# Other order, other PSUM banks and other group sizes in the seven-product up blocks of a hybrid decoder step

## What is computed

```python
def _swiglu(h, w_in, w_out):
    a, b = jnp.split(h @ w_in, 2, axis=-1)
    return (jax.nn.silu(a) * b) @ w_out
...
for i in range(DEPTH):
    x = x + 0.5 * _swiglu(_rmsnorm(x, ln_ffn1[i]), ffn1_w_in[i], ffn1_w_out[i])
    x = x + mixer_i(_rmsnorm(x, ln_mix[i]))
    x = x + 0.5 * _swiglu(_rmsnorm(x, ln_ffn2[i]), ffn2_w_in[i], ffn2_w_out[i])
return _rmsnorm(x, ln_final)
```

## Time and profile before

| | |
|---|---|
| runs (3) | 2259.43, 2260.98, 2261.5 us; median 2260.98 |
| profiled execution | 2256.29 us, span 2254.6 us |
| mean granted TensorE clock | 0.991 |
| busy of the span | PE 97%, VectorE 66%, ScalarE 37% |
| first fast up and down blocks | about 841 to 1243 us of the span |
| second fast up and down blocks | about 1839 to 2240 us |

### The profile page before, as it was taken

How to read it: one execution, slowest core, us unless ns; L and a number is a source line. 1 busy time by engine, 2 the same in 40 slices (tenths; PEclk the granted TensorE clock), 3 DMA queues, 4 the chain that set the end, 5 groups by cost and what they waited for, 6 DMA issues and landing times. The chain is left out here.

```text
span 2254.6 us, 43269 instructions
## 1 busy us (share of the span) xinstructions
PE 2187.2 (97%) x17624; PEld 2148.8 (95%) x17624; DVE 1481.9 (66%) x2218; ACT 828.9 (37%) x1134; POOL 2.2 (0%) x15
## 2 busy tenths in 40 slices
PE   9999999999999789999999999999989999999998
PEld 9999999999999788999999999999988989999998
DVE  5767775467877679758577675234358569668485
ACT  4222232334454445425244322122243345335153
POOL 0000000000000000000000000000000000000000
PEclk9999999999999999999999999999999999999999
DMA  4324543332323225535232322332274424324132
GB/s 137 93 81 121 146 124 96 95 95 72 102 63 91 64 65 142 146 86 143 80 108 61 94 76 78 89 94 76 87 198 159 118 71 132 107 84 141 54 95 81
DMA packets 426648, 227.91 MB, mean 101 GB/s; under 512 B 33473, under 2 KB 419730, under 8 KB 426514
## 3 DMA queue, kind: packets, MB, share of 16 engines
q1 hardware_dynamic: 413986, 212.98, 33.9%
q10 hardware_dynamic: 12528, 13.08, 1.7%
HBM read 206.91 MB, written 23.30 MB: 102 GB/s over the span
## 5 line engine op out<-in xcount | busy, mean ns | idle before, releaser
L2460 PE MATMUL ps<-h_hi,w_hi 128*128 128x288 f32 x1920 | 418.9, 300 | 3.7 <-DVE w_lo L1454 1.9
L2460 PE MATMUL ps<-h_hi,w_lo 128*128 128x288 f32 x1920 | 410.9, 296 | 0.0
L2460 PE MATMUL ps<-h_lo,w_hi 128*128 128x288 f32 x1920 | 410.7, 295 | 0.0
L2592 PE MATMUL ps<-hf_hi,s_hi 128*128 128x288 f32 x1232 | 366.7, 298 | 20.1 <-issue 9.1
L2592 PE MATMUL ps<-hf_lo,s_hi 128*128 128x288 f32 x1232 | 363.0, 295 | 0.0
L2592 PE MATMUL ps<-hf_hi,s_lo 128*128 128x288 f32 x1232 | 362.7, 294 | 0.0
L2460 PEld LDWEIGHTS ps<-h_hi,w_hi 128*128 128x128 f32 x1920 | 308.1, 189 | 13.7 <-issue 5.9
L1454 DVE TENSOR_TENSOR w_lo<-w_raw,w_hi 128x2048 fp32r<-128x2048 f32 (+4 forms) x155 | 267.8, 1731 | 77.4 <-ACT w_hi L911 75.7
L911 ACT ACTIVATE w_hi<-w_raw 128x2048 fp32r<-128x2048 f32 (+4 forms) x155 | 225.9, 1462 | 233.7 <-PE ps L2460 222.5
L2460 PEld LDWEIGHTS ps<-h_lo,w_hi 128*128 128x128 f32 x1920 | 309.2, 189 | 0.0
L2460 PEld LDWEIGHTS ps<-h_hi,w_lo 128*128 128x128 f32 x1920 | 309.1, 189 | 0.0
(11 more groups left out here) (413 smaller groups left out, 3116.4 us busy)
## 6 DMA issues: line engine op xcount, KB each, us to landing
s_raw<-in_ffn_w_in_dram SPq DMA_DIRECT2D x220, 256.0 KB, 3.3
w_raw<-in_ffn_w_in_dram SPq DMA_DIRECT2D x88, 512.0 KB, 5.0
w_raw<-in_hgrn_w_in_dram SPq DMA_DIRECT2D x32, 512.0 KB, 5.4
w_raw<-in_ffn_w_out_dram SPq DMA_DIRECT2D x64, 256.0 KB, 3.1
w_raw<-in_ffn_w_out_dram SPq DMA_DIRECT2D x32, 384.0 KB, 3.9
w_raw<-in_ffn_w_out_dram SPq DMA_DIRECT2D x32, 320.0 KB, 3.6
w_raw<-in_s_w_glu_dram SPq DMA_DIRECT2D x16, 512.0 KB, 5.2
w_raw<-in_ffn_w_out_dram SPq DMA_DIRECT2D x32, 192.0 KB, 2.7
```

The lines of the kernel that those rows point to most:

```text
L2460: ins = M.matmul(ps[:, 2 * b + h, 0:HALF], w[j][:, at:at + P], v[:, k, h * HALF:(h + 1) * HALF], start=k == 0 and n == 0, stop=k == ph.kt ...
L2592: ins = M.matmul(out, w, h, start=f in (0, 1, 3) and k == 0 and n == 0, stop=f in (3, 5, 6) and k == KP - 1 and n == 2, skip_group_check=True)
```

## The change

- Groups of 6, 8, 8 units in place of 8, 8, 6.
- Even units use banks 0, 6, 7, odd ones 3, 1, 2. The second product of a group's first units waits for no down tile any more; the first product of a fast down block now also waits for the last unit's `upper_sum`, which reads banks 1 and 2.
- Last unit of a group: `lower_sum` goes ahead of the split of the down weights, which is parted: buffer 0 behind `lower_sum`, buffer 1 behind `gate_rest`.
- First unit: root and reciprocal go behind `upper_sum`, the token sums behind product 4, ScalarE makes all high parts of the next unit ahead of the Silu.
- Units 0, 1 and 22: sums and rests are moved to earlier tiles of the block before (unit 0: tiles 2 to 6 of `hgrn_out`; its rests of groups 2, 3 and those of unit 22 no longer stand in `form_tile`).
- Fast down blocks have functions of their own, unrolled: the scaling is done in place in PSUM, then the addition frees the banks, and the weights of tile m+2 are split behind the addition of tile m.
- The spreading of taps (`spread_taps`, 8 DMAs each) is shared out 4 and 4 over the first two groups, in place of 6 and 2.

```diff
@@ -42,7 +42,7 @@
 F_GROUPS = (12, 10)
-FAST_GROUPS = (8, 8, 6)
+FAST_GROUPS = (6, 8, 8)
...
@@ -533,7 +533,7 @@
         N_FORM = 2 * KP + 1
-        BANKS = ((0, 1, 2), (3, 6, 7))
+        BANKS = ((0, 6, 7), (3, 1, 2))
...
@@ -554,7 +554,7 @@
         def upper_sums(v):
-            return ps[:, 1:3, 0:HALF] if v % 2 == 0 else ps[:, 6:8, 0:HALF]
+            return ps[:, 6:8, 0:HALF] if v % 2 == 0 else ps[:, 1:3, 0:HALF]
...
@@ -816,9 +816,9 @@
                         load_unit(v)
-                        if v - 2 < 6:
+                        if v < 6:
                             spread_taps(v - 2)
-                        elif 10 <= v < 12:
+                        elif 8 <= v < 12:
...
@@ -1014,13 +1014,14 @@
                         gate_high(vl - 1)
-                    if nxt is not None:
+                    if nxt is not None and v % UNITS:
...
                     if v % UNITS == 0:
+                        unit_high(nxt, 0)
...
@@ -1029,12 +1030,14 @@
                         unit_high(nxt, 2)
+                        if v % UNITS == 0:
+                            unit_high(nxt, 3)
...
                         gate_high(vl)
-                    if nxt is not None:
+                    if nxt is not None and v % UNITS:
...
@@ -1185,13 +1188,12 @@
                     taken = (free[j], i + (ph.tile0 + 1))
-                    if ph.fast:
-                        taken = (x_added, i * 2 + (x_at[ph.name] + j + 1))
                     if r in FORMED:
-                        if (i, j) == (ph.pairs - 1, 1):
-                            for g in range(4):
-                                unit_high(FORMED.index(r) * UNITS, g)
-                        form_tile(r, i * 2 + j, taken)
+                        m = i * 2 + j
+                        if m in (3, 5):
+                            unit_high(0, m - 3)
+                            unit_high(0, m - 2)
+                        form_tile(r, m, taken)
...
@@ -1213,6 +1215,17 @@
+            def fast_down(n, ph):
+                r = MAKES.get((ph.kind, ph.name))
+                for m in range(NK):
+                    i, j = divmod(m, 2)
+                    if m + 2 < NK:
+                        split(ph, j, i + 1, ph, i)
+                    elif m + 2 == NK and n + 1 < len(PH) and not into_sup(n):
+                        split(PH[n + 1], 0, 0, ph, None)
+                    if r is not None:
+                        norm_tile(r, m, (free[j], i + (ph.tile0 + 1)))
...
@@ -1401,13 +1414,12 @@
                         unit_high(UNITS, 0)
-                        unit_high(UNITS, 1)
...
                     if last and j == 1:
-                        unit_high(UNITS, 2)
-                        unit_high(UNITS, 3)
+                        for g in range(1, 4):
+                            unit_high(UNITS, g)
...
@@ -1566,44 +1572,71 @@
+                def normalised(v):
                     dve.wait_ge(post_done, 3 * v + 2)
                     V.tensor_tensor(fca[:], fca[:], rstd[:], ALU.mult).then_inc(post_done, 1)
...
+                def first_unit(v):
+                    if v:
+                        sum_three(v + 1)
+                    unit_rest(v + 1, 0)
+                    if v:
+                        sum_fourth(v + 1)
+                    lower_sum(v)
+                    unit_rest(v + 1, 1)
+                    upper_sum(v)
+                    reciprocal(FORMED[v // UNITS])
+                    normalised(v)
+                    unit_rest(v + 1, 2)
+                    unit_rest(v + 1, 3)
...
                     if v % UNITS == 0:
-                        sum_second(nxt)
-                        reciprocal(FORMED[v // UNITS])
-                        lower_sum(v)
-                        unit_rest(nxt, 0)
-                        sum_fourth(nxt)
-                        upper_sum(v)
-                        unit_rest(nxt, 1)
-                        unit_rest(nxt, 2)
-                        unit_rest(nxt, 3)
+                        first_unit(v)
...
                     if nxt is not None:
-                        sum_second(nxt)
+                        sum_three(nxt)
...
                         unit_rest(nxt, 1)
+                    lower_sum(v)
...
                         rest(down_ph, 0, 0)
-                        rest(down_ph, 1, 0)
-                    lower_sum(v)
                     upper_sum(v)
+                    normalised(v)
...
                         gate_rest(vl)
+                        rest(down_ph, 1, 0)
...
+            def fast_down(n, ph):
+                r = MAKES.get((ph.kind, ph.name))
+                if r is not None:
+                    clear_ssq(r)
+                for m in range(NK):
+                    i, j = divmod(m, 2)
+                    dve.wait_ge(full[j], i + (ph.tile0 + 1))
+                    V.tensor_tensor(pair(j), pair(j), halves(rstd[:]), ALU.mult).then_inc(down_scaled, 1)
+                    dve.wait_ge(down_scaled, x_at[ph.name] + m + 1)
+                    V.scalar_tensor_tensor(out=halves(cols(x, m)), in0=pair(j), scalar=-0.5, in1=halves(cols(x, m)),
+                                           op0=ALU.mult, op1=ALU.add).then_inc(free[j], 1)
+                    if m + 2 < NK:
+                        rest(ph, j, i + 1)
+                    elif m + 2 == NK and n + 1 < len(PH) and not into_sup(n):
+                        rest(PH[n + 1], 0, 0)
+                    if r is not None:
+                        norm_tile(r, m)
...
@@ -2035,19 +2068,19 @@
                     m = i * 2 + j
-                    if r in FORMED and m == NK - 1:
-                        unit_ahead(FORMED.index(r) * UNITS)
+                    if r in FORMED:
+                        if m == 2:
+                            sum_three(0)
+                            sum_fourth(0)
+                        elif m in (4, 6):
+                            unit_rest(0, m - 4)
+                            unit_rest(0, m - 3)
+                        elif m == NK - 1:
+                            sum_three(1)
+                            sum_fourth(1)
                     dve.wait_ge(full[j], i + (ph.tile0 + 1))
-                    if ph.fast:
-                        if j or not isinstance(i, int) or i or x_at[ph.name]:
-                            dve.wait_ge(x_added, i * 2 + (x_at[ph.name] + j))
-                        V.tensor_tensor(halves(ft_s[:]), pair(j), halves(rstd[:]), ALU.mult).then_inc(free[j], 1)
-                        dve.wait_ge(free[j], i + (ph.tile0 + 1))
-                        V.scalar_tensor_tensor(out=cols(x, m), in0=ft_s[:], scalar=-scale, in1=cols(x, m),
-                                               op0=ALU.mult, op1=ALU.add).then_inc(x_added, 1)
-                    else:
-                        V.scalar_tensor_tensor(out=halves(cols(x, m)), in0=pair(j), scalar=scale,
-                                               in1=halves(cols(x, m)), op0=ALU.mult, op1=ALU.add).then_inc(free[j], 1)
+                    V.scalar_tensor_tensor(out=halves(cols(x, m)), in0=pair(j), scalar=scale,
+                                           in1=halves(cols(x, m)), op0=ALU.mult, op1=ALU.add).then_inc(free[j], 1)
...
@@ -2388,7 +2421,11 @@
                     if m == NK - 1:
-                        unit_ahead(UNITS)
+                        sum_three(UNITS)
+                        unit_rest(UNITS, 0)
+                        sum_fourth(UNITS)
+                        for g in range(1, 4):
+                            unit_rest(UNITS, g)
...
@@ -2563,7 +2603,7 @@
                         if f in (0, 2, 4, 6):
-                            pe.wait_ge(s_lo_done, 4 * v + (f // 2 + 1 if formed else (1, 2, 4, 4)[f // 2]))
+                            pe.wait_ge(s_lo_done, 4 * v + f // 2 + 1)
...
@@ -2572,8 +2612,6 @@
                                 pe.wait_ge(post_done, 3 * (v - 2) + 2)
-                            else:
-                                pe.wait_ge(free[1], ph.tile0)
...
@@ -2593,7 +2631,7 @@
                         ins.then_inc(prod_done, 1)
-                        if f == 2 and not formed:
+                        if f == 3 and not formed:
...
@@ -2664,6 +2702,8 @@
                     pe.wait_ge(sd_done, 1)
+                if ph.fast:
+                    pe.wait_ge(post_done, 3 * (FAST.index(ph.name[0]) * UNITS + ph.f0 + ph.kt - 1) + 2)
```

23 lines of the change are left out of this document (11 added, 12 removed).

## The result

The changed kernel takes 2234.03 us (median of 4 runs, 2233.6 to 2239.3) beside 2260.20 us (4 runs) of the kernel before in the same measurement: ratio 0.9889, 95% interval 0.9872 to 0.9906. The forecast was 2237 us, its range 2230 to 2247.

A forecast was written before the change was run, and what follows sets the result against it. TensorE, busy for 97% of the span, was taken as the bound, so only its waits and lost clock could be won. 8.3 + 5.1 + 5.9 + 4.6 = 23.9 us off 2261.0 gave 2237 us, range 2230 to 2247.

The forecast's parts named there:

- What bounds it: Whole kernel: TensorE is busy for 97% of the span, so only its waits or lost clock can be won back.
- Ends of groups, 8.3: Four group ends: product 7 no longer waits for `fc`, 8.9 us, less 0.6 charged for the first down product.
- The rival of 2249: Group ends: the wait only moves to the first down product and its second weights; 2249 us, chance 0.10.
- The clock, 5.1: Three low-clock stretches, two behind group-end waits, one behind the `w_lo` wait at 1245.97, go with those waits: 5.1 us gained.
- The rival that it isn't repeated: Whole kernel: the clock gain is not repeated, as the gate falls at other waits; 2242 us, chance 0.14.
- Down blocks and entry, 5.9: Last down blocks and entry of the next up block: `w_lo` waits and slower starts behind them go, 4.5 and 1.4 us.
- its wide bounds: Fast down tiles: in-place scaling in PSUM taken as 0.76 us from the nearest row, with an upper end of 3.76.
- First units, 4.6: First units: product 3 to product 3 falls to 14.1 us from 17.1 and 15.7, gaining 3.0 and 1.6.
- Now, with F the start of product 3: First units: new chain from product 3 through sums, reciprocal, multiplication, Silu and snapshot to the next product 3, 14.1 us.
- F unchanged, with waits of 1.0 and 0.7: `hgrn_out`: new waits at tiles 4 and 6, yet unit 0's product 3 starts as before, within up to 2 us.
- the 844: End of `hgrn_out`: last addition forecast at 843.3; later than about 844 would show the prediction wrong.
- Against the median: Whole kernel: gain taken from the three-run median, 2261.0 us, 4.7 above the profiled execution's 2256.3.

The follow-up runs named there:

- x2_down: Kernel before with only the new fast down blocks (in-place scaling, weight rest behind the addition), groups still 8, 8, 6: 2254.59 us, ratio 0.9981.
- x3_first: Kernel before with only the new order of the first units (reciprocal behind both sums, token sums behind product 4): 2258.64 us, ratio 0.9997.
- y4_ends: Changed kernel with the order at group ends undone, both rests of the down weights ahead of `lower_sum`: 2245.01 us, ratio 0.9938.
- x1_ends: Kernel before with only `lower_sum` put ahead of the split of the down weights, which is parted, at group ends: 2247.85 us, ratio 0.9959.
- y1_sizes: Changed kernel with groups of 8, 8, 6 again and the taps spread as before: 2234.41 us, ratio 0.9893.
- u2_down: Changed kernel with the old fast down blocks (scaled copy in a buffer, weight rest last), groups still 6, 8, 8: 2236.27 us, ratio 0.9887.
- z2_snap: Changed kernel with the next unit's first snapshot ahead of the Silu and `lower_sum` ahead of a rest, in first units: 2234.79 us, ratio 0.9889.
- y2_banks: Changed kernel with the old PSUM banks and the old waits for them: 2235.57 us, ratio 0.9893.

## Why the prediction was right

**What bounds it:** right. Only TensorE's waits and clock moved. Its busy time fell by 4.7 us of the 22.4. The stretches at the lower clock add up to 38.9 us in the trace of before and 32.9 in that of after, so the clock's loss fell from 19.5 to 16.5, 3.0 us.

**Ends of groups, 8.3, and 3.4 of clock behind two of them:** right in place, size and sum (11.7 forecast; 9.3 to 11.7 alone, 11.0 undone, 12.0 in the traces). The order on DVE came out as drawn, and the wait did not move to the first down product. The rival of 2249 falls. The 0.15 charged at each end for the banks is below what can be measured.

**The clock, 5.1:** the three stretches named did go, with some luck; one of 1.7 came in `hgrn_out`, which the text did not foresee. The rival that it isn't repeated asked how often a wait of 2.1 us at a group's end is followed by a low stretch. The rows of before said two of four. The other profiles with waits of 2.1 us there show two of four each (`x2_down`, `x3_first`) and one of two (`y4_ends`, whose two waits of 1.5 us kept full clock): 7 of 14 in all. The loss also changes its place, in `x2_down` to the end of group 0 of the second fast block, which had full clock before:
```profile
1934.00:1937.40 3.40, 3.40 (x17) 3.40 (x16) 1.63 (x4) 0.68 (x1) 0.00 (x0) 0.51 0.92 264
```
The wait at the entry is followed by a fall in two traces (before, `x3_first`) and not in a third (`x1_ends`). At those rates I estimate the losses at 4 × 7/14 × 1.7 + 2/3 × 1.7 = 4.5 us in a mean run, 0.6 less than the one trace said. Over the runs the mean of time × clock gives 6 us for the clock, but that mixes all stretches, those that cost nothing too.

**Down blocks and entry, 5.9:** the waits were sized right (7.6 forecast with the clock, 8.5 in the traces; the new block alone 4.3 to 5.0), and in-place scaling cost 0.77 us, the taken end of its wide bounds. What the text missed is that it had two reasons for one gain. It wrote "against a product of now 6.3" beside the new order of the weight rest, as if both were needed; `y1_sizes` and `u2_down` show that either does all of it.

**First units, 4.6:** right in size (4.5 in the traces), partly by luck. The step that does not hold as written is "Now, with F the start of product 3": it derived 14.1 us from the new order and compared it with what the old order did before, 15.7 and 17.1. Made alone, the order did give 14.1 and 15.0, but the round behind each became 0.3 to 0.6 longer, and 4.6 did not show in the time. And the old order, too, gets faster under the rest of the change (12.8 and 16.6), so that in the finished kernel the order is worth 0.6 of the 4.5. The step never costed the old chain with the sums of unit 1 out of its way. One reading beside it is wrong as well: from product 3 to the next product 3 it counts "five other products and the token sums", 10.6 us; it is product 3 and six others, 12.1 with the token sums, which is what `z2_snap` shows where it waits for nothing in this round. The sum did not use this figure.

**F unchanged, with waits of 1.0 and 0.7:** where the clock stays full (`y1_sizes`, `y2_banks`), PE idles 0.9 and 0.6 us at tiles 4 and 6, as counted, and 0.2 each at tiles 5 and 7, where the kernel before has 0.8 each. In the changed kernel's own trace the low stretch hides the first of them: it idles 0.8, 0.6 and 0.25 us at tiles 5 to 7. The last addition is at 847.45, not 843.3, and so behind the 844 that the prediction named as a sign of being wrong; but 2.4 of that came in with the stage, and about 1.7 is the low stretch at 810. Without these it is as forecast.

**Against the median.** The profiled execution of before was 4.7 us under its median, and the forecast went to the median by that much. About 2 of it is the faster pace before `hgrn_out`, described below, which that one trace had in its favour and no other has.

## What to carry to other kernels

Ask of each part what it is worth with the others already made: two edits that hide the same queue are worth one, and a chain that looks like an order may be long because of what stands in front of it. Leave-one-out runs and single edits together show this, single edits alone don't. A shorter wait can also spare the clock behind it, while a wait that only moves can take the low clock along: in the fast blocks of these 14 profiles none of 37 waits of 1.0 to 1.8 us was followed by a low stretch, and 16 of 35 of 1.9 to 3.0 us were. What a low stretch costs depends on who is the bound there: 1.7 us at a group's end, nothing in `x1_ends` at units 22 to 24, where the other engines' queue had the time.

## What was not expected of the hardware

- **Matmul pace at full clock differs between executions.** The same stretch of unchanged code, from the views by stretch of the kernel before and the changed one:
```profile
100.00:170.00 70.00, 70.00 (x541) 70.00 (x540) 45.65 (x107) 18.01 (x18) 0.00 (x0) 1.00 0.30 82
```
```profile
100.00:170.00 70.00, 70.00 (x528) 70.00 (x527) 45.69 (x107) 18.20 (x18) 0.00 (x0) 1.00 0.28 76
```
  541 matmuls against 528 in 70 us, both at a granted clock of 1.00: 130.0 ns from start to start between 97 and 172 us in the profiled execution of before, 133.3 ns in the changed kernel and in every other one of the study, and in that first one too elsewhere. It is 1.9 us that no instruction explains; the cause stays open.
- **Low stretches wander.** Those at group ends, at the entry and in the first units all lie at a wait of PE, but of 14 waits of 2.1 us at a group's end 7 had one. The Trainium skill, TensorE: Matmul & The Clock Gate (Part 1, "What's actually happening"), has the gate look at the engine's activity with a phase that is not tied to the kernel. By that rule, the traces agree as far as the waits at group ends go: the same wait of the same length is followed by a low clock in one execution and by full clock in the next. The wait at 807 to 810 us is no such case, since it was longer where the clock fell.
